# Attention in units of four heads, 0/1 slot products after the experts, and sparse-attention parameters through GpSimd's queue, in a two-block fp32 transformer kernel

## What is computed

```python
s = jnp.where(mask, s.astype(jnp.float32) * scale, NEG)
p = jax.nn.softmax(s, axis=-1)
o = gates[:, :, 0] * o_cmp + gates[:, :, 1] * o_slc + gates[:, :, 2] * o_win
```

## Time and profile before

| | us |
|---|---|
| median of 3 runs (lowest, highest) | 2770.07 (2763.48, 2772.11) |
| the profiled execution's own time | 2773.9 |
| its span in the trace | 2772.1 |
| TensorE matmuls busy | 2370.4 (86% of the span) |
| VectorE busy | 1805.9 (65%) |
| ScalarE busy | 1363.3 (49%) |
| GpSimd busy | 61.9 (2%) |
| mean granted TensorE clock | 0.905 of 2.4 GHz |

### The profile page before, as it was taken

How to read it: one execution, slowest core, us unless ns; L and a number is a source line. 1 busy time by engine, 2 the same in 40 slices (tenths; PEclk the granted TensorE clock), 3 DMA queues, 4 the chain that set the end, 5 groups by cost and what they waited for, 6 DMA issues and landing times.

```text
span 2772.1 us, 43460 instructions
## 1 busy us (share of the span) xinstructions
PE 2370.4 (86%) x16356; PEld 2191.3 (79%) x16356; DVE 1805.9 (65%) x1977; ACT 1363.3 (49%) x1553; POOL 61.9 (2%) x100
## 2 busy tenths in 40 slices
PE   5669999678669999685979978686999999999997
PEld 4559999577559999584879978575899999999996
DVE  4457676333557676584456658454888888888885
ACT  3326555223426554243443333442777777777774
POOL 0000000000000000100000010000000000000000
PEclk8779999885679999895999998697999999999999
DMA  6228999350028999440525564041899999999993
GB/s 209 78 77 313 355 368 332 97 173 0 18 76 328 351 370 339 130 151 18 161 88 187 164 174 137 31 152 31 303 315 343 366 346 343 353 357 339 347 365 112
DMA packets 340151, 609.64 MB, mean 220 GB/s; under 512 B 15680, under 2 KB 271488, under 8 KB 315328
## 3 DMA queue, kind: packets, MB, share of 16 engines
q1 hardware_dynamic: 329696, 590.84, 61.2%
q0 software_dynamic: 4800, 12.99, 2.0%
q10 hardware_dynamic: 5408, 2.27, 0.3%
HBM read 605.02 MB, written 1.05 MB: 219 GB/s over the span
## 4 chain that ended last, share of the span: by engine, by line
PE 76%; DVE 12%; ACT 4%; issue 4%; DVEq 2%; POOLq 1%; DMA 1%; POOL 1%; ACTq 0%; PEldq 0%
PE psum L129 15%; PE psum L131 14%; PE psum L130 14%; PE psum L1830 9%; PE psum L1866 9%; PE psum L722 2%; PE psum L1854 2%; DVE h_cf L2634 2%; PE psum L2326 2%; PE psum L307 1%; ACT scores L745 1%; PE psum L711 1%; PE psum L699 1%; POOLq L210 1%; PE psum L2164 1%
## 5 line engine op out<-in xcount | busy, mean ns | idle before, releaser
L1595 DVE TENSOR_TENSOR weight_ring_rounded<-weight_ring,weights_high_rounded 128x2048 fp32r<-128x2048 f32 x264 | 604.1, 2291 | 95.2 <-ACT weights_high_rounded L1590 95.0
L1590 ACT ACTIVATE weights_high_rounded<-weight_ring 128x2048 fp32r<-128x2048 f32 x264 | 504.8, 1915 | 104.5 <-PE psum L131 97.0
L129 PE MATMUL psum<-weights_high_rounded,scores_rounded 128*128 128x256 f32 x1408 | 406.3, 289 | 11.6 <-DVE scores_rounded L1627 10.9
L131 PE MATMUL psum<-weights_high_rounded,scores_rounded 128*128 128x256 f32 x1408 | 398.8, 283 | 0.0
L130 PE MATMUL psum<-weight_ring_rounded,scores_rounded 128*128 128x256 f32 x1408 | 398.4, 283 | 0.0
L1924 DVE TENSOR_TENSOR weight_ring_rounded<-weight_ring,weights_high_rounded 128x2048 fp32r<-128x2048 f32 x128 | 292.7, 2292 | 94.9 <-ACT weights_high_rounded L1919 94.9
L129 PEld LDWEIGHTS psum<-weights_high_rounded,scores_rounded 128*128 128x128 f32 x1408 | 270.1, 192 | 16.8 <-DVE scores_rounded L1627 12.7
L1830 PE MATMUL psum<-weights_high_rounded,scores_rounded 128*128 128x256 f32 x1024 | 262.5, 294 | 13.5 <-DVE scores_rounded L2003 11.8
L130 PEld LDWEIGHTS psum<-weight_ring_rounded,scores_rounded 128*128 128x128 f32 x1408 | 270.3, 192 | 3.4
L131 PEld LDWEIGHTS psum<-weights_high_rounded,scores_rounded 128*128 128x128 f32 x1408 | 270.0, 192 | 0.0
L131 PE MATMUL psum<-weights_high_rounded,xT_rounded 128*128 128x512 f32 (+3 forms) x688 | 261.8, 381 | 0.0
(11 more groups left out here) (476 smaller groups left out, 4160.0 us busy)
## 6 DMA issues: line engine op xcount, KB each, us to landing
weight_ring<-in_moe_w_gate_dram SPq DMA_DIRECT2D x152, 1024.0 KB, 6.3
weight_ring<-in_moe_w_up_dram SPq DMA_DIRECT2D x152, 1024.0 KB, 8.3
weight_ring<-in_moe_w_down_dram SPq DMA_DIRECT2D x152, 1024.0 KB, 7.9
weight_ring<-in_w_in_dram SPq DMA_DIRECT2D x20, 1024.0 KB, 6.2
weight_ring<-in_ffn_w_gate_dram SPq DMA_DIRECT2D x11, 1024.0 KB, 5.3
weight_ring<-in_ffn_w_up_dram SPq DMA_DIRECT2D x11, 1024.0 KB, 5.4
weight_ring<-in_ffn_w_down_dram SPq DMA_DIRECT2D x11, 1024.0 KB, 5.0
weight_ring<-in_w_out_dram SPq DMA_DIRECT2D x8, 1024.0 KB, 5.0
```

The lines of the kernel that those rows point to most:

```text
L129: nc.tensor.matmul(out, lh, rh, start=start, stop=False)
L131: return nc.tensor.matmul(out, ll, rh, start=False, stop=stop)
L1590: self.c.nc.scalar.activation(ring.high(self.s0 + q, 1, SLOT), ring.view(self.p0 + q, 1, SLOT), ACT.Copy).then_inc(ring.high_ready, 1)
L1595: self.c.nc.vector.tensor_tensor(ring.low(self.p0 + q, 1, SLOT), ring.view(self.p0 + q, 1, SLOT), ring.high(self.s0 + q, 1, SLOT).bitcast( ...
```

## The change

1. `attention` works in units of four heads, `units = [(j, h)]`. TensorE makes the scores of two units ahead, in two pairs of PSUM banks; the product with the values comes two groups of transposes late; there are four buffers of `scores` and three of `probs_turned`. A group of transposes waits for its own heads' exponentials (`probs.at(g + 1)`). VectorE finishes unit u-3 after the pass over unit u.
2. Products with the values are 128 columns wide for all calls: each writes its own 64 columns and 64 beyond, which the next head's first product overwrites. Value tiles get 64 columns more, of zeros.
3. Where a unit is long and has a bias, the mask or bias, the scale, the sign and the row's extreme are made by one `tensor_tensor_reduce` for each head (4 for a unit, with two drains) in place of one pass and one reduction; the exponential takes scale -1. Where the recurrence is long, the product with the decay and the row sum are made the same way. The forgetting attention's scale moves into the copy of q.
4. NSA's two calls become one of 16 units, in the order group, branch, token tile 1, then 0 (two long units, two short ones). The gate is multiplied into the reciprocals (`weight`) and the other branch is added after each unit (`then`); the join between the calls and the gate stage with its join are gone.
5. Sparse experts: `spread` is the transposed 0/1 matrix G, fp32r, made on TensorE before the gather, in the same stage. The slots' weights are summed by eight fp32 products of one column after the gather and copied by VectorE. The transpose stage and its join are gone. After the loop each group of transposed outputs is scaled by its slots' weights and rounded by ScalarE (high), VectorE makes the low part, and 32 fp32r products of 512 columns follow, mixed with the transposes; the join between is gone. `meanwhile` now stands ahead of ScalarE's and VectorE's part.
6. NSA's parameters: the seven DMAs are issued on GpSimd's queue, and VectorE and TensorE wait for them where they are used.

```diff
@@ attention: TensorE
+    AHEAD, LAG, PTS = 2, 2, 3
-            if j >= 1:
-                pe.wait_ge(*scaled.at(j))
+            if u >= 2:
+                pe.wait_ge(*scaled.at(u - 1))
...
+            pe.wait_ge(*probs.at(g + 1))
             if g >= 2:
                 pe.wait_ge(*copied.at(g - 1))
...
             pe.wait_ge(*copied.at(g + 1))
-            if j >= 2:
-                pe.wait_ge(*written.at(j - 1))
+            if u >= 2:
+                pe.wait_ge(*written.at(u - 1))
             for a, (i, s) in enumerate(blocks):
-                last = nc.tensor.matmul(c.psum[:, 6 + j % 2, i * dv:(i + 1) * dv], PT[:, g % 2, a * P:(a + 1) * P],
-                                        v(b, i, s), start=(s == 0), stop=(s == kts[j] - 1))
+                at = i * dv
+                wide = v(b, 4 * h + i, s)
+                last = nc.tensor.matmul(c.psum[:, 6 + u % 2, at:at + P], PT[g % PTS][:, a * P:(a + 1) * P],
+                                        wide, start=(s == 0), stop=(s == kts[j] - 1))
...
+        for u in range(min(AHEAD, len(units))):
+            scores(u)
+        for g in range(len(groups)):
+            turn(g)
+            u = groups[g][0]
+            if g == of_unit[u][0] and u + AHEAD < len(units):
+                scores(u + AHEAD)
+            if g >= LAG:
+                pv(g - LAG)
@@ attention: ScalarE
+        split(act, "act", ahead[:1])
+        if gated is None:
+            for part in range(len(of_unit[0])):
+                exps(0, part)
+        for u in range(len(units)):
+            mine = of_unit[u]
+            more = len(of_unit[u + 1]) if gated is None and u + 1 < len(units) else 0
+            for x, g in enumerate(mine):
+                act.wait_ge(*turned.at(g + 1))
+                if g >= PTS:
+                    act.wait_ge(*pv_group.at(g - PTS + 1))
+                nc.scalar.activation(PT[g % PTS], c.psum[:, 4 + g % 2, :], ACT.Copy).then_inc(*copied.up())
+                for part in range(x * more // len(mine), (x + 1) * more // len(mine)):
+                    exps(u + 1, part)
+            if u == len(units) // 2 - 1:
+                split(act, "act", ahead[1:])
@@ attention: VectorE
+            elif signs[u] < 0:
+                for i in range(4):
+                    nc.vector.tensor_tensor_reduce(dst[:, i, :], sc[:, i, :], bias(t, h, nk)[:, i, :], -scale, 3e38,
+                                                   ALU.add, ALU.min, neg_max[:, u % 4, i:i + 1])
+                dve.drain().then_inc(*scaled.up())
+                maxed.up()
+                dve.drain().then_inc(maxed.sem, 1)
...
+            if u == len(units) - 1:
                 split(dve, "dve", ahead)
-            if j >= 1:
-                finish(j - 1)
-        finish(len(batches) - 1)
+            if u >= 3:
+                finish(u - 3)
+        for u in range(max(0, len(units) - 3), len(units)):
+            finish(u)
@@ nsa_mixer
-    load_params(c, [(gate_b[:, :], bcast(arg["c_gate_b"][0])),
+    load_ahead(c, "mixer_params_landed", [(gate_b[:, :], bcast(arg["c_gate_b"][0])),
...
+    def add(dve, t, b, h, written):
...
+        dve.wait_ge(*written.now())
+        c.dve(nc.vector.tensor_tensor(o, o, (oc, osel)[branch][:, t, at], ALU.add))
+    attention(c, [(t, (branch, g)) for g in range(NSA_G) for branch in range(2) for t in (1, 0)], NSA_HPG, NSA_D,
@@ sparse_experts, before the loop
+        for s in range(SLOTS // P):
+            ss = slice(s * P, (s + 1) * P)
+            for t in range(TT):
+                last = nc.tensor.transpose(c.psum[:, 6 + s // 2, (s % 2) * TOK + t * P:(s % 2) * TOK + (t + 1) * P], G[:, t, ss].bitcast(F32), c.ident[:, :])
+        last.then_inc(*spread_turned.up())
...
+                last = nc.tensor.matmul(c.psum[:, 0, s:s + 1], GW[:, t, ss], c.ones[:, 0:1], start=(t == 0), stop=(t == TT - 1))
+        last.then_inc(*slots_summed.up())
...
-    transpose_stage(c, [([GW[:, t, s * P:(s + 1) * P] for s in (2 * g, 2 * g + 1) for t in range(TT)],
-                         spread[:, 2 * g:2 * g + 2, :].rearrange("p s t -> p (s t)"), ("act", "dve")[g]) for g in range(2)])
@@ sparse_experts, after the loop
+        def turn(s):
+            for h in range(2):
+                g = 2 * s + h
+                if g >= 4:
+                    pe.wait_ge(*slots_low.at(g - 3))
+                for k in range(4):
+                    last = nc.tensor.transpose(c.psum[:, 4 + g % 4, k * P:(k + 1) * P], outT[:, 4 * h + k, s * P:(s + 1) * P], c.ident[:, :])
...
+                    for a, rows in enumerate((rows_high, rows_low)):
+                        last = nc.tensor.matmul(c.psum[:, 2 * t + h, :], spread[:, s, t * P:(t + 1) * P], rows[:, s, h, :],
+                                                start=(s == 0 and a == 0), stop=(s == SLOTS // P - 1 and a == 1))
...
+        turn(0)
+        turn(1)
+        for s in range(SLOTS // P):
+            mix(s)
+            if s + 2 < SLOTS // P:
+                turn(s + 2)
...
+            nc.scalar.activation(rows_high[:, s, h, :], c.psum[:, 4 + g % 4, :], ACT.Copy, scale=slot_w[:, s:s + 1]).then_inc(*slots_high.up())
...
+            nc.vector.scalar_tensor_tensor(rows_low[:, s, h, :], c.psum[:, 4 + g % 4, :], slot_w[:, s:s + 1],
+                                           rows_high[:, s, h, :].bitcast(F32), ALU.mult, ALU.subtract).then_inc(*slots_low.up())
@@ hybrid_mixer
+    scaled_copy = lambda dst: (lambda r: nc.scalar.activation(dst, r, ACT.Copy, scale=FX_D ** -0.5))
-              scale=FX_D ** -0.5, bias=lambda t, b, nk: decay(df, FX_H, t))
+              scale=1.0, bias=lambda t, h, nk: decay(df, FX_H, t)[:, 4 * h:4 * h + 4])
```

272 lines of the change are left out of this document (154 added, 118 removed).

## The result

The changed kernel takes **2692.64 us** (median of 4 runs, 2686.56 to 2695.11) against 2769.53 for the kernel before beside it: a ratio of 0.9722, 95% interval 0.97 to 0.9745. The forecast was 2690, range 2672 to 2732. The profiled execution has a span of 2690.6 us, 81.5 less than before, and a mean granted clock of 0.93 (0.905 before).

A forecast was written before the change was run, and what follows sets the result against it. TensorE held three quarters of the wait chain; in the attentions engines took turns at a low clock. Savings 42 + 12 + 18.9 - 3.3 + 10.5 = 80 us from the median 2770.07 gave 2690 us, range 2672 to 2732.

The forecast's parts named there:

- NSA's attention: NSA's two calls, join and gates: 105.8 us become 64 with 16 overlapping units, 42 saved.
- MLA: MLA's attention: 23 to 26 us against 27.2, unit 2's value products waiting for unit 0's finish; 3 saved.
- forgetting, both: Two forgetting attentions, starting at the lower clock: 22.5 to 27 us against 25.9; 2.5 saved, twice.
- recurrence, both: Two recurrences of two units: only second score products and fused pass help; 1.5 us saved twice, bounds 0 and 3.
- after the expert loops: Expert loop's end to next stage: 20.0 us become 12.9; 7.1 saved in first and third calls, 4.7 in second, together 18.9.
- before the expert loops: Around the gather, three calls: the stage grows from 3.0 to 4.2 us; 3.3 lost in all, bounds nothing and 6.
- NSA's parameters: NSA's projection: without ScalarE's parameter wait, TensorE's 8.15 us idle goes, plus 2.5 for slow products behind it; 10.5 saved.
- The pair: NSA's attention: one long and one short unit take 6.6 us with waits, TensorE 6.15, VectorE 5.7, ScalarE 5.3.
- with scores made two units ahead, that wait should find its products done: NSA's attention: VectorE's finish of unit u-3 should not wait for TensorE's value products; no separate size given.
- a sign of being wrong: Attentions: the forecast is wrong if the clock reads near 0.5 or VectorE idles between passes waiting for value products.
- Rival 1: Attentions: the clock stays at 1.2 GHz, NSA saves only 8 us, sum 36, total 2734; chance 0.15.
- Rivals 2 to 4: Whole kernel: queues lock step, 2705 us, chance 0.15; units run serially, about 2812, 0.02; weight ring bounds, about 2765, 0.02.

The follow-up runs named there:

- the later finish: The changed kernel with VectorE's finish one unit later in NSA's attention (unit u-4, eight sets of row sums): 2693.41 us.
- width: The kernel before with only the products with the values made 128 columns wide (last head of eight stays 64): 2742.61 us, ratio 0.9899 to the kernel before.
- units: The changed kernel with the products with the values 64 columns wide again, all else as changed: 2704.77 us.
- the seven traces: Traces keeping the change's place for VectorE's splits, its wide products and fused instruction; MLA's attention 23.9 to 26.1 us, first forgetting attention 22.2 to 26.0.
- the spread splits: The changed kernel with VectorE's two weight splits moved within the attention, after the middle unit's pass and between the last finishes: 2684.33 us.
- one other move: Splits after the second expert loop put behind the slots' rows; with splits spread in four-unit attentions, against the changed kernel: 2678.26 us.

## Why the prediction was right, and where its steps were not

The total was 2.6 us off, and better than its parts: that it is so near is luck. Most terms were put too high, by 12.6 us together, and two that were put too low, the recurrence and the stages before the loops, gave 9.5 back. Terms in us, by the first profile of the changed kernel and (in brackets) the second:

```
                        predicted   measured
NSA's attention            42       39.0 (39.0)
MLA                         3        1.6 (1.7)
forgetting, both            5        1.5 (0.2)
recurrence, both            3        9.2 (9.2)
cross, both                 1        0.9 (0.0)
after the expert loops     18.9     16.4 (16.6)
before the expert loops    -3.3      0
NSA's parameters           10.5      8.4 (10.4)
sum                        80       77.0 (77.1)
```

The span fell by 81.5 (78.7); what is left over lies in stages that the change leaves alone, the first expert loop above all (285.6 before, 283.0 and 284.8 after).

- **NSA's attention.** The mechanism held: fewer gaps, the upper clock (0.94), the fused instruction at its 0.42. The pair was mis-sized: 7.43 us where the step took 6.6. TensorE's work in it was 6.4, near the 6.15; the waits between units are 1.0, not 0.45. The step "with scores made two units ahead, that wait should find its products done" failed: VectorE waited 2.39 us for them in each period. The prediction had named this wait as a sign of being wrong. But the later finish showed that this wait is worth only 2 us in all; the greater one is copy, exponentials, transposes at a short unit, which the prediction did not lay out in order. Filling and end took 7.1 us (66.6 less four periods of 14.87) instead of 11, which gave back more than half of the pair's error.
- **The clock.** Rival 1 is out: 0.94. The choice of width as the likely cause was half right: the four kernels of the table (neither, width, units, both) show that each of width (10.0 and 7.3 us) and units with what came with them (31.7 and 29.0) gives its part in NSA's attention, nearly independent of the other. From 638.5 to 668.3 the granted clock was 1.00, with 24 of 104 matrix instructions in each period transposes. Transposes alone even raised it. In the kernel before TensorE idled 9.82 us and then ran nothing but sixteen transposes of the layer's input; the clock was 0.50 in the first 2.57 us of them and 1.00 behind them:

```profile
523.93 3.33 PE L307 MATMUL psum<-ident,x 128*128 128x128 f32 x16 [9.82 <-DVE x L409]
...
523.93:526.50 2.57, 2.57 (x12) 2.57 (x13) 1.70 (x2) 0.60 (x1) 0.00 (x0) 0.50 0.00 0
527.00:528.30 1.30, 0.26 (x4) 0.03 (x2) 0.69 (x1) 0.39 (x1) 0.04 (x1) 1.00 0.00 0
```

The second profile of the changed kernel shows the same: 0.50 to 516.5 us, 1.00 from 517.3. So the rule of the Trainium skill ("TensorE: Matmul & The Clock Gate", Part 4), that the upper clock does not engage for transpose mode, does not hold for the transposes of this kernel (`nc.tensor.transpose` of fp32), and what kept the clock down from 672 to 681 was not that transposes stood among the products; the narrow products are what the runs point to.
- **MLA and forgetting.** Predicted 3 and 5, measured 1.6 and 1.5. The step had named the queue (the finish of unit 0 behind the passes and both splits) and priced it too low: it cost some 4.5, 3.5 and 4.7 us on the mean of the seven traces, as the spread splits show (20.1 to 21.9, and 21.1 twice), and most of it where the clock fell behind the wait too: in the one trace in which it stayed up (a wait of 1.11 us) the first forgetting attention took 22.2.
- **Recurrence.** 1.5 each predicted, bounds 0 and 3, measured 4.6 each, outside the bounds. The step counted instructions at the old clock: before, the whole stage ran at 0.50, after at 0.82. The width is not the reason (9.8 with narrow products), and the fused instruction is about 0.9 of it.
- **After the loops.** 7.1 predicted for the first and third call, 6.7 measured in each. Both sides of the sum were short: from the first transpose to the next stage it was 20.5 us before (20.0 in the prediction) and 13.9 after (12.9). The second: 4.7 predicted, 3.0 and 3.3 measured in two profiles, 4.6 and 4.7 in two others in which the clock fell less. That was 17.5 and 17.2 us where about 15 was to be seen. The cover that was gone was named; that the wait costs the clock as well was not.
- **Before the loops.** Predicted to lose 1.1 each, lost nothing: from the gather stage's first instruction to the loop's first product 17.42 us for 17.41. The step's prices held: transposes 1.6, column sums 1.8, copy and join 0.5, together 3.9 (4.2 predicted) for the 3.0 that went. The term that it put at nothing was the gather. Behind the transposes it ran at a mean clock of 0.90 for 0.82 and took 8.6 us for 9.5.
- **The parameters.** The wait went whole. 10.5 predicted; 10.4 in one profile, 8.4 in the other. The difference is when the clock rose: within the input's transposes in the one, so that the unsplit products took 8.61 us, and only within the unsplit products in the other, 10.49 us.
- **Rivals 2 to 4.** Lock step was there in part (1.33 and 0.63 us of waiting in each period) at less than its price, and not from the uneven order. No stage got slower by the units running in series, and the ring of weights never became the bound.

Some 2 us were given back where the change does nothing: the join before the first hybrid mixer waits for parameters that GpSimd loads. The last landed 6.4 us after its issue, 4.5 in the kernel before and 4.3 in that with width alone. It was so with the old expert layers (6.3) and with the parameters by ScalarE (7.6) too, but not with the fused instruction undone (4.4). Why the same transfers took longer stays open; it wasn't tried.

## What to carry to other kernels

Before crediting a new order of work, ask what each engine does *last* in its queue: here work put ahead of the last finishes took back some 4 us in each of three attentions, and moving it gave 14 us together with one other move. Here a stall of 2.2 to 2.6 us in TensorE was followed by the lower clock, so price a wait with the slower instructions behind it. Where a change has two causes, run all four kernels (neither, each alone, both); the width alone, a few lines, gave about a third of the gain.

## What the hardware showed that was not expected

- Value products of 128 columns where 64 are needed cost next to nothing: a group of four blocks (x8) took 1.06 to 1.16 us at the upper clock, a narrow one 1.00 to 1.10, and at the lower clock four narrow blocks took 1.81 us and eight wide ones 3.58. They raised the mean granted clock from 0.57 to 0.74 in NSA's selected branch and from 0.78 to 0.94 between the two kernels with units.
- Sixteen transposes alone, after 9.8 us of idle time, brought TensorE from the lower clock to the upper (at 523.93 in the kernel before).
- The granted clock differs between executions of one program in the same place: the same 32 unsplit products took 10.49 and 8.61 us. Single stages thus vary by 2 to 4 us (MLA's attention 23.9 to 26.1, the first forgetting attention 22.2 to 26.0 in kernels that don't differ there).
- fp32 products of one column take as long as those of 64: the eight column sums (sixteen instructions) took 1.84 us, 0.115 an instruction, at the upper clock, and sixteen instructions of 64 columns 2.00.
- The fused instruction of VectorE on 256 columns from PSUM starts every 0.35 us, with 0.08 us for reading its accumulator between, so four take 1.46 us where a pass and a reduction took 2.5.
